# Latents of four more sequences laid out in blocks by transfers on chip and turned by VectorE, in a two-layer hybrid decoder step

## The reference

```
def mla_sample_attention(q_nope, q_rope, c_kv, k_rope, w_uk, w_uv, lat_past, kr_past):
    q_lat = einsum('bqhd,chd->bqhc', q_nope, w_uk)
    s_past = einsum('bqhc,bkc->bhqk', q_lat, lat_past) + einsum('bqhr,bkr->bhqk', q_rope, kr_past)
    ...
    p = softmax(s)
    ctx = einsum('bhqk,bkc->bqhc', p[..., :past], lat_past) + ...
```

## Time and profile before

| | us |
|---|---|
| median of 3 runs | 1265.94 (1265.73 to 1266.15) |
| profiled execution, its time | 1266.02 |
| profiled execution, its span | 1264.2 |
| PE busy in it | 1250.9 |
| VectorE / ScalarE / GpSimd busy | 549.7 / 250.5 / 153.0 |

### The profile page before, as it was taken

How to read it: one execution, slowest core, us unless ns; L and a number is a source line. 1 busy time by engine, 2 the same in 40 slices (tenths; PEclk the granted TensorE clock), 3 DMA queues, 4 the chain that set the end, 5 groups by cost and what they waited for, 6 DMA issues and landing times.

```text
span 1264.2 us, 18049 instructions
## 1 busy us (share of the span) xinstructions
PE 1250.9 (99%) x7142; PEld 1022.8 (81%) x7142; DVE 549.7 (43%) x1387; ACT 250.5 (20%) x640; POOL 153.0 (12%) x210
## 2 busy tenths in 40 slices
PE   8999999999999999999999999999999999999997
PEld 6878777776888888888888787777778888888886
DVE  7866646323235333321178746463241453324212
ACT  3432414311100111110033324243111011111000
POOL 2012442010000000020001134511000000000000
PEclk9999999999999999999999999999999999999999
DMA  9433576357454444464454344755564544444440
GB/s 342 155 100 101 134 254 227 130 188 170 122 152 148 147 143 147 148 225 150 148 154 142 100 115 150 249 205 177 140 173 126 149 143 149 150 150 150 151 138 35
DMA packets 93971, 198.49 MB, mean 157 GB/s; under 512 B 41680, under 2 KB 42736, under 8 KB 91072
## 3 DMA queue, kind: packets, MB, share of 16 engines
q1 hardware_dynamic: 84624, 156.15, 40.4%
q0 software_dynamic: 8768, 40.84, 9.4%
q10 hardware_dynamic: 496, 0.36, 0.1%
HBM read 183.86 MB, written 9.25 MB: 153 GB/s over the span
## 4 chain that ended last, share of the span: by engine, by line
PE 95%; DVE 4%; ACT 1%; issue 0%; DMA 0%; SPq 0%; DVEq 0%; ACTq 0%
PE banks L573 77%; PE banks L1063 2%; PE banks L1076 1%; PE banks L1111 1%; PE banks L1074 1%; PE banks L968 1%; PE banks L717 1%; DVE arena L1715 1%; PE banks L996 1%; PE banks L675 0%; PE banks L1012 0%; DMA arena<-in_x 0%; DVE arena L2114 0%; PE banks L873 0%; PE banks L590 0%
## 5 line engine op out<-in xcount | busy, mean ns | idle before, releaser
L573 PE MATMUL banks<-arena 128*128 128x264 f32 x4512 | 1032.3, 388 | 5.7 <-DVE arena L1609 4.9
L573 PEld LDWEIGHTS banks<-arena 128*128 128x128 f32 x4512 | 851.0, 190 | 169.2 <-issue 13.2
L1217 ACT ACTIVATE arena<-banks 128x256 f32<-128x256 f32 (+8 forms) x252 | 92.6, 391 | 403.7 <-PE banks L573 293.2
L2217 DVE TENSOR_SCALAR arena<-arena 128x256 f32<-128x256 f32 x44 | 18.2, 414 | 130.2 <-ACT arena L1217 130.0
L2250 DVE SCALAR_TENSOR_TENSOR arena<-banks,arena 128x264 f32<-128x264 f32 x16 | 6.9, 433 | 134.2 <-PE banks L573 134.2
L2431 POOL COPY arena<-arena 128x2 f32<-128x2 f32 x44 | 13.7, 310 | 377.6 <-ACT arena L1217 275.9
L1248 ACT ACTIVATE arena<-banks 128x264 f32<-128x264 f32 x32 | 12.6, 392 | 130.6 <-PE banks L573 130.6
L2110 DVE COPY arena<-banks 128x512 f32<-128x512 f32 x24 | 16.6, 690 | 36.7 <-PE banks L1063 36.5
L1529 ACT ACTIVATE arena<-arena 128x256 f32<-128x256 f32 x44 | 18.4, 417 | 66.3 <-DVE arena L2219 66.3
L2224 DVE SCALAR_TENSOR_TENSOR arena<-arena 128x256 f32<-128x256 f32 x44 | 18.7, 426 | 26.6 <-ACT arena L1529 26.6
L2229 DVE TENSOR_TENSOR arena<-arena,banks 128x256 f32<-128x256 f32 x42 | 17.7, 422 | 26.4 <-PE banks L573 26.3
(11 more groups left out here) (447 smaller groups left out, 1072.5 us busy)
## 6 DMA issues: line engine op xcount, KB each, us to landing
arena<-in_weights SPq DMA_DIRECT2D x229, 512.0 KB, 3.6
arena<-in_weights SPq DMA_DIRECT2D x113, 256.0 KB, 3.5
arena<-in_s POOLq DMA_DIRECT2D x2, 2048.0 KB, 10.9
out_ss_o<-arena POOLq DMA_DIRECT2D x16, 256.0 KB, 3.1
arena<-in_mla_w POOLq DMA_DIRECT2D x4, 1024.0 KB, 6.7
arena<-arena SPq DMA_DIRECT2D x64, 64.0 KB, 2.4
arena<-in_c POOLq DMA_DIRECT2D x4, 512.0 KB, 6.3
out_sc_o<-arena POOLq DMA_DIRECT2D x16, 128.0 KB, 3.8
```

The costliest lines, as they stand in the source:

```text
L573: mm = nc.tensor.matmul(dst, ring[:, at_:at_ + 128], rhs[:, j, :], start=(start and j == 0), stop=(stop and j == k - 1))
L1217: return A(dst, src, ACT.Copy, scale=scale)
L2217: link(ts(cv, fc[:, j % 3, 0:TP], w[0], par[:, Q_FB + j:Q_FB + j + 1], ALU.mult, ALU.add))
```

## The change

Sequences 0, 1, 4 and 5 take the way that 6 and 7 had; 2 and 3 keep PE's transposes. The blocks of 0, 1, 4 and 5 are written into `ltt[:, n % 2]` itself, and VectorE turns them in place. SP's copies of a sequence stand in front of a marked weight unit, waiting for what frees the target: 0 and 1 for the last "uq", 4 for sequence 2 scored, 5 for sequence 3 scored, 6 and 7 for `cx` 0 as before. In VectorE's order `turn(n, parts)` does the keys and the transposes: sequence 0 after `divided(0)`, 1 after `divided(1)`, 4 between `total(0)` and `newest(0)`, 5 after `combined(0)`, 6 three half pieces later, 7 another five later. GpSimd's gathers of 5 to 7 wait for a scored sequence instead of for transposes.

```
     def mark(*sequences):
+        at_ = (34 + piece[0]) // 2 + SLOTS - 1
+        for n in sequences:
+            while at_ in marks:
+                at_ += 1
+            marks[at_] = n
...
+    mark(0, 1)
     add("uq", 8, "V"); add("bcK", 4, "V")
...
-        if n < 6:
+        if n in (2, 3):
             s.extend(("ltr", 4 * n + i, "AV"[i % 2]) for i in range(4))
...
+    mark(4)
+    add("ss"); half(1); ...; half(3); add("lsum", 1, "V"); mark(5); add("cx")
+    mark(6, 7)
...
+        def blocks(n):
+            return lat[n - 6] if n >= 6 else ltt[:, n % 2].rearrange("p i n -> p (i n)")
...
             def blocks_of_latents(l, n):
-                sp.wait_ge(*out(l, "cx", 0))
+                if n < 2:
+                    sp.wait_ge(*out(l, "uq", 7))
+                elif n == 5:
+                    sp.wait_ge(*out(l, "ss", 0))
+                elif n == 4:
+                    sp.wait_ge(*at(l, "page_scored", 3))
+                else:
+                    sp.wait_ge(*out(l, "cx", 0))
...
-                if u % UNITS in (BLOCKS_AT, BLOCKS_AT + 1):
-                    blocks_of_latents(u // UNITS, 6 + u % UNITS - BLOCKS_AT)
+                if u % UNITS in BLOCKS_AT:
+                    blocks_of_latents(u // UNITS, BLOCKS_AT[u % UNITS])
...
-                        pe.wait_ge(*at(l, "lat_turned", 4 * (n - 5)))
+                        pe.wait_ge(*at(l, "lat_turned", 4 * (n - 1 if n >= 4 else n + 1)))
...
+                def turn(n, parts):
+                    if parts[0] == 0:
+                        dve.wait_ge(*at(l, f"lat_in{n}", 32))
+                        if n >= 2:
+                            dve.wait_ge(*scored(n - 2))
+                        V.transpose(krt[:, n % 2, :], key[n]).then_inc(*up("key_turned"))
+                        dve.wait_ge(*at(l, f"lat_blocks{n}", 256))
+                    for i in parts:
+                        V.transpose(ltt[:, n % 2, i, :], blocks(n)[:, 512 * i:512 * i + 512]).then_inc(*up("lat_turned"))
...
                 divided(0)
-                half(4)
+                turn(0, (0, 1)); half(1); turn(0, (2, 3)); half(3)
                 divided(1)
-                half(5)
+                turn(1, (0, 1)); half(2); turn(1, (2, 3)); half(3)
...
-                for n in range(4):
+                half(2)
+                for n in (2, 3):
                     pages(n)
                 top(0, 1)
                 half(3)
                 total(0)
+                turn(4, (0, 1, 2, 3))
                 newest(0)
                 half(2)
                 combined(0)
-                pages(4); half(2); pages(5); half(4); pages(6); pages(7)
+                turn(5, (0, 1, 2, 3)); half(1); half(2)
+                turn(6, (0, 1, 2, 3)); half(5)
+                turn(7, (0, 1, 2, 3)); half(2)
                 top(1, 2)
...
                 for n in range(5, NB):
-                    pool.wait_ge(*out(l, "ltr", 4 * (n - 4) + 3))
+                    pool.wait_ge(*at(l, "page_scored", n - 4))
```

More of the change, by code:

```diff
@@ L98, in schedule, with mark @@
 def schedule():
-    s, piece = [], [0]
+    s, piece, marks = [], [0], {}
+    def mark(*sequences):
+        at_ = (34 + piece[0]) // 2 + SLOTS - 1
[3 more added lines that the diff above has]
+            marks[at_] = n
     def add(name, n=1, reader="A", first=0):
@@ L149, in schedule @@
         pages(n)
-    add("ss"); half(1); add("mxT", 1, "V"); half(1); add("mxB", 1, "V"); half(3); add("lsum", 1, "V"); add("cx")
-    at_context = (34 + piece[0]) // 2
+    mark(4)
+    add("ss"); half(1); add("mxT", 1, "V"); half(1); add("mxB", 1, "V"); half(3); add("lsum", 1, "V"); mark(5); add("cx")
+    mark(6, 7)
     half(2); add("cmb", 1, "V")
@@ L160, in schedule @@
     add("fd", 8, "V")
-    return s, at_context + SLOTS - 1
+    return s, marks
 SCHED, BLOCKS_AT = schedule()
@@ L171, in turn_banks @@
 def turn_banks():
-    first_page = {("ltr", 0): ("ss", 0), ("ltr", 16): ("ss", 1)}
+    first_page = {("ltr", 8): ("ss", 0), ("cmb", 0): ("ss", 1)}
     early = {e[0] for e in EARLY}
@@ L201 @@
     decay_masked=1, diag_set=3, ffn_conv=22, ffn_sconv=2, ffn_stanh=2, ffn_tail=22, ffn_tanh=22, ffn_zeros=1, fh_loaded=16,
-    hidden=2, hidden_norm=16, norm_raw=16, norm_square=16, norm_sum=14, hist_loaded=16, key_copied=2, key_turned=8, lat_turned=8, **{f"lat_blocks{n}": 256 for n in (6, 7)}, **{f"lat_in{n}": 32 for n in range(8)},
+    hidden=2, hidden_norm=16, norm_raw=16, norm_square=16, norm_sum=14, hist_loaded=16, key_copied=2, key_turned=8, lat_turned=24, **{f"lat_blocks{n}": 256 for n in (0, 1, 4, 5, 6, 7)}, **{f"lat_in{n}": 32 for n in range(8)},
     inverse=1, inverse_turned=1, m_loaded=64, mdecay_exp=1, mdecay_in=4, mdecay_masked=1, merged=8, mla_q=16, mla_kv=16,
@@ L458, in build @@
         last_rms = bank("fd", 1)[:, 0:TT]
+        def blocks(n):
+            return lat[n - 6] if n >= 6 else ltt[:, n % 2].rearrange("p i n -> p (i n)")
         def quarter_of_latents(n, b, q):
-            return (lat[n - 6][32 * q:32 * q + 32, 512 * b:512 * b + 512].rearrange("i (r j) -> i r j", r=NR),
+            return (blocks(n)[32 * q:32 * q + 32, 512 * b:512 * b + 512].rearrange("i (r j) -> i r j", r=NR),
                     lat[n][32 * b:32 * b + 32, :].rearrange("i (r q j) -> i r q j", r=NR, q=4)[:, :, q, :])
@@ L1070, in pages @@
                     else:
-                        pe.wait_ge(*at(l, "lat_turned", 4 * (n - 5)))
+                        pe.wait_ge(*at(l, "lat_turned", 4 * (n - 1 if n >= 4 else n + 1)))
                     for i in range(4):
-                        turned = heads(ltt[:, n % 2, i, :], 32) if n >= 6 else turned_lat(n)[:, :, 32 * i:32 * i + 32]
+                        turned = heads(ltt[:, n % 2, i, :], 32) if n not in (2, 3) else turned_lat(n)[:, :, 32 * i:32 * i + 32]
                         nc.tensor.matmul(heads(sb[32 * i:32 * i + 32, :], 32), ql_pad[:, g, s_, :], turned,
@@ L1471, in pages @@
                 def pages(n):
-                    for i in (0, 2):
+                    for i in (0, 2) if n in (2, 3) else ():
                         act.wait_ge(*out(l, "ltr", 4 * n + i))
@@ L2050, in _, with scored @@
                 last.then_inc(*up("query_blocks"))
+                def scored(n):
+                    if n % 4 == 3:
+                        return out(l, "ss", n // 4)
+                    return at(l, "page_scored", 3 * (n // 4) + n % 4 + 1)
+                def turn(n, parts):
[7 more added lines that the diff above has]
+                        V.transpose(ltt[:, n % 2, i, :], blocks(n)[:, 512 * i:512 * i + 512]).then_inc(*up("lat_turned"))
                 def masked(g):
@@ L2084, in _ @@
                 divided(0)
-                half(4)
+                dve.wait_ge(*at(l, "st_pc", 32))
+                dve.wait_ge(*at(l, "st_sn", 32))
+                dve.wait_ge(*at(l, "st_conv", 16))
+                turn(0, (0, 1))
+                half(1)
+                turn(0, (2, 3))
+                half(3)
                 divided(1)
-                half(5)
+                turn(1, (0, 1))
+                half(2)
+                turn(1, (2, 3))
+                half(3)
                 dve.wait_ge(*out(l, "sn"))
@@ L2091, in _ @@
                 V.tensor_copy(ckb, heads(bank("ckB")[0:32, 0:2 * P], P)).then_inc(*read("ckB"))
[L2092 to L2100, removed]
                 def pages(n):
                     dve.wait_ge(*at(l, f"lat_in{n}", 32))
-                    if n >= 2:
-                        dve.wait_ge(*scored(n - 2))
+                    dve.wait_ge(*scored(n - 2))
                     V.transpose(krt[:, n % 2, :], key[n]).then_inc(*up("key_turned"))
[L2107 to L2114, removed]
+                    for i in (1, 3):
+                        dve.wait_ge(*out(l, "ltr", 4 * n + i))
+                        V.tensor_copy(ltt[:, n % 2, i, :], bank("ltr", 4 * n + i)).then_inc(*read("ltr", 4 * n + i))
                     half(1)
@@ L2158, in _ @@
                 combined(0)
-                pages(4)
+                turn(5, (0, 1, 2, 3))
+                half(1)
                 half(2)
[L2161 to L2164, removed]
+                turn(6, (0, 1, 2, 3))
+                half(5)
+                turn(7, (0, 1, 2, 3))
+                half(2)
                 top(1, 2)
```

## The result

The changed kernel takes 1296.05 us, median of 4 runs (1294.61 to 1298.62), beside 1266.05 (1265.73 to 1266.74) for the kernel before on the same chip: ratio 1.0238 [1.0221, 1.0256]. It is slower by 30.0 us. I forecast 1282, range 1271 to 1288: the sign was right, the size was little more than half of what came, and the time lies outside my range. The profiled execution took 1296.58 us, with a span of 1294.8.

The account below looks back on a forecast made before the run. TensorE (PE), busy 1250.9 of 1264.2 us, was taken to bound the kernel. Per layer, 6.05 us later despite the transposes gone plus 1.95 for the clock; two layers add 16.0 to 1266.02, giving 1282, range 1271 to 1288.

Parts of the forecast that it names:

- What is taken from PE: Sequences 0, 1, 4 and 5 lose their PE transposes: 7.02 us saved a layer, 14.0 in all.
- What is put on SP, sequences 4 to 7: Four copy groups of 11.32 us in a row make PE wait before 5, 6, 7; each layer 6.05 us later.
- the sum: Whole kernel: 2 x (6.05 + 1.95) = 16.0 us added to the profiled 1266.02 us, giving 1282.
- The clock before sequence 7: PE's clock falls during the 6.4 us wait, doubling sequence 7's scoring: 1.95 us a layer, upper bound 3.8.
- Sequences 0 and 1: Start of each layer: copies arrive nearly in time, VectorE's reads of "wa" slightly late; loss 0.3 us a layer.
- 201.0 + 11.3 = 212.3: Layer 0's first copy group on SP: starts after the last "uq" at 201.0, takes 11.3 us, ends at 212.3.
- Sequence 1 late: Rival at VectorE: sequence 1's blocks there after 230.2 hold "wa" 3 and PE, 2 us per us; 1286, chance 10%.
- the copies stay hidden: Faster rival: SP copies in a long row go at 0.40 us, groups take 6.4, nothing late; 1252.6, chance 7%.
- its turning point: SP copy pace at which the change's sign turns between faster and slower: 0.61 us a copy.
- the ring runs dry: SP's late weight units in the eight-unit ring hold PE: no price while PE waits for blocks first; left in range.
- 4.4 us for a sequence: Estimate from the skill page for one sequence's 1 MB of copies; with it nothing would be late.

Follow-up runs that it names:

- experiment 3: Changed kernel, but GpSimd gathers sequences 2 and 3 only after the blocks of sequence 1 have landed: 1285.34 us, ratio 1.0147 to the kernel before.
- experiment 5: Changed kernel with late gathers of 2 and 3, each copy in 32 runs of 2 KB instead of 512 of 128 bytes (scores not the reference's): 1275.43 us.
- 9: Changed kernel with late gathers of 2 and 3, only 8 of 16 copies made for each of sequences 4 to 7 (stale blocks): 1251.52 us, ratio 0.9886.
- experiment 8: Changed kernel with late gathers of 2 and 3, plus 12 unread PE products before the wait for sequence 7: 1281.02 us, against 1285.07 without the products.
- Experiment 1: Changed kernel with sequences 4 and 5 back on PE's transposes, so only 0 and 1 newly by blocks: 1271.95 us, ratio 1.0043 to the kernel before.
- Experiment 4: Changed kernel with keys of sequences 2 and 3 gathered as before, only their latents after sequence 1's blocks landed: 1285.07 us, ratio 1.0148.

## Why the prediction was right in sign and wrong in size

**What is taken from PE:** right. 64 transposing matmuls are left, and where no blocks are late (half copies), 7.6 and 7.1 us a layer come back, against 7.02 worked out.

**What is put on SP, sequences 4 to 7:** right. Eight groups took 10.7 to 12.5, mean 11.4 (11.32 in the sum). From the start of the half piece before sequence 0 to the end of sequence 7, PE lost 7.6 and 8.6 us net, against 7.7. The waits before 5, 6 and 7 were 3.6, 1.5 and 6.2 us (3.1, 3.4 and 5.1 in layer 1), against 2.7, 3.8 and 6.4, and the second came through the bank of "wc", as said. Experiments 3, 5 and 9 show that these groups set PE's waits: with shorter groups the waits in layer 0 sum to 6.1 us instead of 9.3, and with half of the copies there are none.

**The clock before sequence 7:** right in kind. Sized at 1.95 a layer; scoring took 1.4 and 1.8 us longer (3.37 and 3.73 against 1.95). Without it experiment 8 came out 4.0 faster over two layers; there the half piece behind had been slow too. But it fell in more places than the sum had. Against the same work before, PE's matmuls took 3.0 and 1.8 us longer behind the waits at "wa", 1.6 behind sequence 5 (layer 0), 1.7 behind "wc" (layer 1), 1.4 and 1.8 at sequence 7 and 0.3 behind it: 11.6 in all, where the sum had 3.9. What was lost so at 5 and 6 was swallowed by the wait for 7, as said; what was lost at "wa" wasn't.

**Sequences 0 and 1: the step that failed.** "201.0 + 11.3 = 212.3" priced the first group by groups that had the transfer engines nearly for themselves. This one met two gathers of 1 MB each and took 20.0 and 18.1 us. The second then ended at 233.7 instead of 224.8, its blocks reached VectorE at 235.6 instead of 226.5, and instead of 0.3 a layer the stretch lost 8.4 and 5.6 us: the waits of 0.67 and 4.22 (3.52 in layer 1) and what the clock took after them. From the start of the late piece to sequence 0 it was 251.34 - 237.30 = 14.0 us, against 242.91 - 231.86 = 11.05 for the same work before: 3.0 us. The term was sized at 0.6 for both layers and measured 14.0, 13.4 more, and 1282 + 13.4 is 1295.4. Experiment 1, with this part alone, is 6.2 us slower although 7.0 were taken off PE, which makes 13.2. When the gathers move away (experiment 3), only 10.4 us of the total comes back: the row of four then costs 19.6 us of the total, against 15.4 in my sum (12.1 and 3.9, less 0.6). Its waits are not longer (22.7 us over both layers, 23.1 in the kernel after); the matmuls behind them are: the 32 records behind sequence 5 took 8.47 and 8.03 us instead of 7.29, the 16 behind sequence 7 4.78 and 4.96 instead of 3.73 and 4.04. Why the clock stayed low for longer there is open. The rival "Sequence 1 late" had the place and the mechanism, but I bounded its price by groups of 11.60 and left out that the clock falls there as it does before 7. The overlap could have been seen: GpSimd's gathers of 2 and 3 were in flight at the very time at which SP was to start, and I had used the key gather's row for its landing alone.

**The rivals.** That the copies stay hidden is refuted by the groups' lengths; its turning point, 0.61 us a copy, agrees with what was measured on both sides of it: at 0.63 to 0.70 (experiment 5) the kernel is still 9.5 us slower, and with half as many copies it is 14.4 us faster. That the ring runs dry isn't seen: every wait in the sequences ends with VectorE. The Trainium skill (DMA: Bandwidth & Descriptors, "Issuing engines are not separate DMA queues") has two rules that these runs weigh. That initiating is usually small beside the DMA isn't borne out for these copies: they cost SP 0.70 us each, for 64 KB and for 32 KB, and those of 64 KB landed 2.4 us after their issue. That all issuers share the same engines, and that a second one saves only issuing time, is borne out: 0.49 us a copy instead of 0.70, and no more, with the engines at 0.89. The section "Anatomy of one DMA" of the same page of the Trainium skill, from which the prediction took 4.4 us for a sequence, is about a single transfer issued by GpSimd; the sixteen that SP issues took 10.7 and more.

**What stays open:** why a group beside gathers grows by 7 to 9 us, whether by bytes or by the order in which the engines take packets of the two queues. Experiment 4 shows only that it is the latents' gathers, and the stretch 217 to 219 (engines at 0.34, a copy of 2.46 us) that full engines don't explain every slow copy.

## What to carry to other kernels

Price a transfer by its neighbours in time: a row of the trace holds for a new place only if what the other queues move there is the same. Where work goes from a full engine to a queue, write out when the queue has delivered each part, since four groups of 11.3 us, for uses some 8 us apart (sequences 4 to 7 were scored at 286.87, 296.03, 307.02 and 311.08 before), make a loss of a saving, and three of them don't. And a wait of some us on TensorE can cost more than its length, since the matmuls behind it may run at the lower clock, as they did in most cases here.

## What was unexpected of the hardware

- Where no gather ran beside it, SP needed 0.63 to 0.80 us, on average over a group, for each copy from SBUF to SBUF, whether it has 64 KB in runs of 128 bytes (10.7 to 12.8 us for 16), in runs of 2 KB (10.0 to 11.1), or half the bytes (20.9 to 22.5 for 32).
- Such copies lose much to gathers: the 16 took 18 to 20 us beside 2 MB of gathered latents. Single ones in that stretch, from SP's timeline of the kernel after:

```profile
206.99 3.36 SPq L524 DMA_DIRECT2D arena<-arena  x1
...
213.88 2.34 SPq L524 DMA_DIRECT2D arena<-arena  x1
```

- Two issuers of such copies came to 0.49 us a copy, and SP's own fell to 1.33 us a copy while GpSimd's went on at 0.65 (16 in 10.37 us).
- The length of the last wait alone doesn't tell whether TensorE comes out of it at the lower clock. In layer 1 of the kernel after, the 8 matmuls behind 3.52 us of waiting took 3.73 us (1.2 GHz), those of scoring behind 3.06 us took 1.07 (2.4 GHz); in experiment 3, scoring behind 2.95 us took 1.94.

```profile
874.73 3.73 PE L593 MATMUL banks<-arena 128*128 128x264 f32 x8 [3.52 <-DVE arena L1819]
...
937.33 1.07 PE L1094 MATMUL banks<-arena 128*32 128x512 f32 x8 [3.06 <-DVE arena L2086]
```
